# An encoder trunk on one core: the MLP's first product takes both parts of the activations as one 512-column operand

## The chip, the core and the metric

The kernel runs on one core of a Trainium2 chip. The metric is the device time of one launch in microseconds. TensorE (PE in the profile; its weight loads are PEld) multiplies into PSUM, ScalarE (ACT) and VectorE (DVE) read PSUM and work on SBUF, GpSimd (POOL) does small work on SBUF, and SyncE (SP) issues the DMAs that bring the weights in from HBM.

## The reference, cut to what matters

Two layers (`DEPTH` = 2) over 256 tokens of width 1024: four token mixers with gates, then an MLP with 4096 hidden features. The change is in the MLP.

```python
for l in range(DEPTH):
    h = rms_norm(x, norm1_g[l])
    ...                                   # projections, four mixers, gates
    x = x + jnp.sum(g * y, axis=2) @ w_o[l]

    h2 = rms_norm(x, norm2_g[l])
    x = x + jnp.square(jax.nn.relu(h2 @ w_ff1[l])) @ w_ff2[l]
return rms_norm(x, final_g)
```

## The kernel before

**Products of split numbers.** Every large product is made of three float32r matmuls: each operand is split into a high part (rounded to float32r) and a low part (what is left), and hi·hi, hi·lo and lo·hi are added up in PSUM. `split_product` issues the three for each block of 128 contracted features; each takes its stationary operand anew. In the trace the three are lines L1179, L1180 and L1181.

**Weights.** A layer's weights come in 64 chunks (`CHUNKS`) of 1 MB, each in two halves. SP loads a half into `raw` (a ring of two chunks), ACT rounds it into `w_hi` (L572, `split_hi`), DVE subtracts into `w_lo` (L806, `split_lo`), and PE uses the chunk from a ring of four (`RING`). SP may load chunk c's half only when DVE is through with that half of chunk c-2, and ACT may write `w_hi` of chunk c only when PE is through with chunk c-4 (`w_used`). A layer's last chunks stand in the order f1 14, f2 13, f1 15, f2 14, f2 15, and the next layer's chunks 0 and 1 follow.

**The MLP.** There are 16 chunks f1 of 256 hidden features and 16 chunks f2 (`FF_N` = 16). The product in (`mlp_in`) of chunk i has the weights as its stationary operand and the activations `act_hi`, `act_lo` (256 tokens) as the moving one: 2 feature blocks (d) x 8 contraction blocks (kc) x 3 matmuls = 48 matmuls of 256 columns, into one half of a PSUM bank for each d (`bank_w[:, i % 2]`; for chunk 0 `bank_w` and `bank_o`). DVE then makes `relu` (L1036: maximum with 0, times `root_row`, which carries the norm's factor of each token), ACT squares it into `part_hi` (L701), DVE squares it into `sq` (L1042) and subtracts into `part_lo` (L1045). The product out (`mlp_out`) of chunk i adds 24 matmuls of 512 columns into the four banks of `bank_acc`, the sums of the whole layer.

**The order.** It is written out by hand, engine by engine. PE: `mlp_in(0)` (in `mlp_in_first`), a matmul that turns `rstd` into a row (L1420, into `bank_x`), `mlp_in(1)`, `mlp_out(0)`, `mlp_in(2)`, `mlp_out(1)`, ... `mlp_in(15)`, `mlp_out_last`. The last one goes by pieces (two token tiles x two halves of the width, 6 matmuls each): pieces 0 and 1 of chunk 14, then pieces 0 and 1 of chunk 15, then 2 and 3 of chunk 14, 2 of chunk 15, the first transposes of the next layer (`turn_h`, L1190), and piece 3 of chunk 15. In the loop ACT and DVE split chunk f1 i+1, do the MLP work of chunk i, and split chunk f2 i; behind the loop they split f2 15 and then do the MLP work of chunk 15. Then they split chunks 0 and 1 of the next layer, and only then does DVE add the sums to `xs` (`residual`, L845), from which the next norm is made (ACT sums squares, POOL makes `rstd`, DVE and ACT scale into `h`), for which `turn_h` waits.

## Time and profile before

| | us |
|---|---|
| three timed runs: median | 841.54 |
| lowest, highest | 841.27, 841.65 |
| the profiled execution | 843.16 |
| its span, first to last instruction | 841.4 |
| granted TensorE clock over the span | 0.995 of full speed |

The profile shows one execution. It took 843.16 us, 1.76 us over its own span and 1.62 us over the median of the timed runs; durations are read inside the span, and a difference worked out from them is put against either time alike. The busy time of a matmul in the profile overlaps the next one's, so what a matmul costs in a stream is the distance between two starts.

### The profile page before, as it was taken

To read this page: it belongs to the slowest core of one execution; us is meant where nothing else is said; L and a number is where in the kernel's file an instruction comes from. 1 tells how busy PE (TensorE), PEld (TensorE's weight loads), DVE (VectorE), ACT (ScalarE), POOL (GpSimd) and SP (SyncE) were. 2 spreads that over 40 slices of the span, in tenths; PEclk is the share of its full clock that TensorE was granted. 3 is DMA by queue.
4 is the path that set the end of the run, shared out by engine and by line. 5 is a ranking of instruction groups with operands and counts; after the bars stand their busy time and mean duration, and the time that the engine had idled before them with its cause. 6 is when DMAs were issued, how large, how long until landed. Compare 5 with 4: busy or idle time off the path is not lost.

```text
span 841.4 us, 14859 instructions
## 1 busy us (share of the span) xinstructions
PE 821.5 (98%) x5781; PEld 754.2 (90%) x5781; DVE 538.2 (64%) x781; ACT 410.8 (49%) x698; POOL 80.8 (10%) x105
## 2 busy tenths in 40 slices
PE   6899999999999999999999999999999999999997
PEld 6899988999889999999989999889997999999995
DVE  4586665966667556665568756677756865556663
ACT  5345566645465334444364566466454643334442
POOL 4030000202210000000033000002211100000000
PEclk9899999999999999999999999999999999999999
DMA  9566643364337655555566654343353655655541
GB/s 283 179 190 198 175 126 101 103 199 142 110 106 245 200 199 181 178 175 184 184 184 203 214 166 143 125 132 119 114 171 125 212 195 194 199 199 187 170 142 50
DMA packets 100850, 141.09 MB, mean 168 GB/s; under 512 B 4796, under 2 KB 87040, under 8 KB 100800
## 3 DMA queue, kind: packets, MB, share of 16 engines
q1 hardware_dynamic: 99296, 137.12, 51.1%
q0 software_dynamic: 1216, 3.17, 1.6%
q8 instruction: 34, 0.56, 0.3%
q10 hardware_dynamic: 288, 0.11, 0.1%
q14 instruction: 16, 0.13, 0.0%
HBM read 139.33 MB, written 1.05 MB: 167 GB/s over the span
## 4 chain that ended last, share of the span: by engine, by line
PE 79%; issue 12%; POOL 4%; DVE 3%; DMA 1%; ACT 1%; POOLq 0%; ACTq 0%; DVEq 0%
PE bank_w L1179 16%; PE bank_w L1181 16%; PE bank_w L1180 16%; PE bank_acc L1179 8%; PE bank_acc L1180 8%; PE bank_acc L1181 8%; POOL mix L542 3%; PE bank_acc L1275 2%; DVE w_lo L806 1%; PE bank_acc L1287 1%; PE bank_o L1304 1%; DMA raw<-in_w_in 1%; PE bank_w L1171 1%; DMA cst<-in_table 1%; PE bank_x L1252 0%
## 5 line engine op out<-in xcount | busy, mean ns | idle before, releaser
L806 DVE TENSOR_TENSOR w_lo<-raw,w_hi 128x1024 fp32r<-128x1024 f32 (+1 forms) x256 | 308.5, 1254 | 48.2 <-ACT w_hi L572 48.0
L1179 PE MATMUL bank_w<-act_hi,w_hi 128*128 128x256 f32 x1008 | 287.9, 286 | 0.0
L1181 PE MATMUL bank_w<-act_hi,w_lo 128*128 128x256 f32 x1008 | 285.8, 284 | 0.0
L1180 PE MATMUL bank_w<-act_lo,w_hi 128*128 128x256 f32 x1008 | 285.3, 283 | 0.0
L572 ACT ACTIVATE w_hi<-raw 128x1024 fp32r<-128x1024 f32 (+1 forms) x256 | 256.7, 1060 | 29.0 <-DMA raw<-in_w_in 18.4
L1179 PEld LDWEIGHTS bank_w<-act_hi,w_hi 128*128 128x128 f32 x1008 | 191.6, 190 | 7.1 <-ACT big L693 3.1
L1180 PEld LDWEIGHTS bank_w<-act_lo,w_hi 128*128 128x128 f32 x1008 | 190.9, 189 | 1.8 <-issue 0.5
L1181 PEld LDWEIGHTS bank_w<-act_hi,w_lo 128*128 128x128 f32 x1008 | 191.2, 190 | 0.0
L701 ACT ACTIVATE part_hi<-big 128x512 fp32r<-128x512 f32 x32 | 20.2, 633 | 194.2 <-DVE big L1036 191.5
L1179 PE MATMUL bank_acc<-w_hi,part_hi 128*128 128x512 f32 x256 | 100.3, 392 | 0.0
L1180 PE MATMUL bank_acc<-w_lo,part_hi 128*128 128x512 f32 x256 | 100.2, 392 | 0.0
L1181 PE MATMUL bank_acc<-w_hi,part_lo 128*128 128x512 f32 x256 | 99.8, 390 | 0.0
L1036 DVE SCALAR_TENSOR_TENSOR big<-bank_w,root_row 128x512 f32<-128x512 f32 x30 | 20.7, 691 | 117.4 <-PE bank_w L1181 117.4
L1179 PE MATMUL bank_w<-w_hi,act_hi 128*128 128x268 f32 x256 | 75.1, 293 | 5.7 <-ACT qkv L609 5.5
L1181 PE MATMUL bank_w<-w_hi,act_lo 128*128 128x268 f32 x256 | 74.4, 291 | 0.0
L1180 PE MATMUL bank_w<-w_lo,act_hi 128*128 128x268 f32 x256 | 74.2, 290 | 0.0
L693 ACT ACTIVATE big<-bank_w,vec_all 128x256 f32<-128x256 f32 x64 | 26.9, 471 | 84.3 <-PE bank_w L1181 84.3
L542 POOL TENSOR_TENSOR mix<-mix,tmp 128x512 f32<-128x512 f32 x24 | 35.5, 1489 | 255.5 <-DVE tmp L1021 255.2
L1181 PEld LDWEIGHTS bank_acc<-w_hi,part_lo 128*128 128x128 f32 x256 | 48.1, 188 | 10.6
L1179 PEld LDWEIGHTS bank_acc<-w_hi,part_hi 128*128 128x128 f32 x256 | 48.1, 188 | 9.5
L1180 PEld LDWEIGHTS bank_acc<-w_lo,part_hi 128*128 128x128 f32 x256 | 48.0, 188 | 8.9
L1179 PEld LDWEIGHTS bank_w<-w_hi,act_hi 128*128 128x128 f32 x256 | 49.4, 193 | 6.0 <-issue 6.0
(180 smaller groups left out, 987.3 us busy)
## 6 DMA issues: line engine op xcount, KB each, us to landing
raw<-in_w_ff SPq DMA_DIRECT2D x128, 512.0 KB, 4.8
raw<-in_w_gate SPq DMA_DIRECT2D x64, 512.0 KB, 4.7
raw<-in_w_in SPq DMA_DIRECT2D x32, 536.0 KB, 5.6
raw<-in_w_o SPq DMA_DIRECT2D x16, 512.0 KB, 4.5
raw<-in_w_branch SPq DMA_DIRECT2D x16, 256.0 KB, 4.4
raw<-in_w_branch SPq DMA_DIRECT2D x8, 512.0 KB, 4.6
xs<-in_x SPq DMA_DIRECT2D x2, 512.0 KB, 4.6
out_y<-big SPq DMA_DIRECT2D x4, 256.0 KB, 2.1
```

The costliest lines, as they stand in the source:

```text
L542: nc.gpsimd.tensor_tensor(mix[:, k % 4, :], mix[:, k % 4, :], tmp[:, k % 2, :], ALU.add).then_inc(mixed, 1)
L572: nc.scalar.activation(half_view(w_hi, c, h), raw_half(c, h), ACT.Copy).then_inc(w_hi_ready, 1)
L693: ins = nc.scalar.activation(big[:, i % 8, d * SEQ:(d + 1) * SEQ], bank[:, d * SEQ:(d + 1) * SEQ], ACT.Tanh, bias=vec(BG + 2 * i + d, l), ...
L701: nc.scalar.activation(part_hi[:, b, :, :].rearrange("p k s -> p (k s)"), relu[b], ACT.Square).then_inc(u_hi_ready, 1)
L806: nc.vector.tensor_tensor(half_view(w_lo, c, hf), raw_half(c, hf), f32(half_view(w_hi, c, hf)), ALU.subtract).then_inc(w_lo_ready, 1)
L1036: ins = nc.vector.scalar_tensor_tensor(out=relu[b].rearrange("p (d s) -> p d s", d=2), in0=bank_w[:, b, :].rearrange("p (d s) -> p d s", d ...
L1171: nc.tensor.matmul(bank_w[:, 1, 0:P], ident, ident, start=True, stop=True)
L1179: nc.tensor.matmul(dst, s_hi, m_hi, start=first, stop=False)
L1180: nc.tensor.matmul(dst, s_hi, m_lo, start=False, stop=False)
L1181: ins = nc.tensor.matmul(dst, s_lo, m_hi, start=False, stop=last)
L1275: ins = nc.tensor.matmul(bank_acc[:, half, keys], q[:, t * P:(t + 1) * P], k, start=True, stop=True)
L1287: ins = nc.tensor.transpose(bank_acc[:, 2 + b, at:at + P], prob[:, b, t, kt * P:(kt + 1) * P], ident)
```

## The change

Chunk i of the MLP's product in now has 4 half banks instead of 2. `act_hi` and `act_lo` become the two halves of one tile `act[:, kc, m, :]`, so that high and low part of a contraction block lie side by side. `wide_product` then issues two matmuls instead of three: w_hi times both parts (512 columns, a whole bank: the left half gets hi·hi, the right half w_hi·act_lo) and w_lo times the high part (256 columns, onto the left half). Both halves have to be added afterwards. ACT copies the right halves of the two banks into `relu` (`u_copy`), DVE adds the left halves (`u_summed`), and the rest follows from SBUF. The banks of odd chunks are `bank_o` and `bank_x`, so `mlp_in(1)` waits until ACT has copied `root_row` out of `bank_x`. DVE's MLP work is cut in two (`mlp`: add, relu, square; `mlp_lo`: the subtraction), and the splits of f2 chunks stand between the two parts; on ACT they stand between `u_copy` and the square.

```diff
-        act_hi = sb("act_hi", [P, KD, SEQ], F32R)
-        act_lo = sb("act_lo", [P, KD, SEQ], F32R)
+        act = sb("act", [P, KD, 2, SEQ], F32R)
+        act_hi, act_lo = (act[:, :, m, :] for m in range(2))
...
-        bank_w = ps("bank_w", [P, 2, 512])
+        bank_u = ps("bank_u", [P, 4, 512])
+        bank_w, bank_o, bank_x = bank_u[:, 0:2, :], bank_u[:, 2, :], bank_u[:, 3, :]
...
+            def u_copy(i, l, g=0):
+
+                b = i % 2
+                act.wait_ge(w_used, used_count(l, POS["f1", i], g))
+                if i >= 2:
+                    act.wait_ge(u_squared, l * FF_N + 2 * g + (i - 1))
+                nc.scalar.activation(relu[b].rearrange("p (d s) -> p d s", d=2), bank_u[:, 2 * b:2 * b + 2, SEQ:2 * SEQ],
+                                     ACT.Copy).then_inc(u_copied, 1)
...
-                split_hi(POS["f2", 0], l)
+                split_hi_half(POS["f2", 0], 0, l)
                 act.wait_ge(root_turned, l + 1)
                 nc.scalar.activation(root_row[:, :], bank_x[:, 0:SEQ], ACT.Copy).then_inc(root_row_ready, 1)
+                u_copy(0, l)
+                split_hi_half(POS["f2", 0], 1, l)
                 mlp(0, l)
                 with act.Fori(0, MLP_TURNS) as g:
                     for i in (1, 2):
                         split_hi(POS["f1", i] + AHEAD - 1, l, g)
+                        u_copy(i, l, g)
+                        split_hi(POS["f2", i - 1] + AHEAD - 1, l, g)
                         mlp(i, l, g)
-                        split_hi(POS["f2", i - 1] + AHEAD - 1, l, g)
+                u_copy(FF_N - 1, l)
                 split_hi(POS["f2", FF_N - 1], l)
                 mlp(FF_N - 1, l)
...
+                banks = bank_u[:, 2 * b:2 * b + 2, :]
+                u = relu[b].rearrange("p (d s) -> p d s", d=2)
+                dve.wait_ge(u_copied, l * FF_N + 2 * g + (i + 1))
+                nc.vector.tensor_tensor(u, u, banks[:, :, 0:SEQ], ALU.add).then_inc(u_summed, 1)
+                dve.wait_ge(u_summed, l * FF_N + 2 * g + (i + 1))
                 if i == 0:
                     dve.wait_ge(root_row_ready, l + 1)
...
                 dve.wait_ge(relu_ready, l * FF_N + 2 * g + (i + 1))
                 nc.vector.tensor_tensor(sq[b], relu[b], relu[b], ALU.mult).then_inc(u_squared, 1)
+
+            def mlp_lo(i, l, g=0):
...
+                mlp(FF_N - 1, l)
                 split_lo(POS["f2", FF_N - 1], l)
-                mlp(FF_N - 1, l)
+                mlp_lo(FF_N - 1, l)
...
+            def wide_product(dst, sides, start, stop, lo_counts=None):
+
+                for k, (s_hi, s_lo, m) in enumerate(sides):
+                    if lo_counts is not None:
+                        pe.wait_ge(h_lo_ready, lo_counts[k])
+                    first, last = start and k == 0, stop and k == len(sides) - 1
+                    nc.tensor.matmul(dst, s_hi, m.rearrange("p m s -> p (m s)"), start=first, stop=False)
+                    ins = nc.tensor.matmul(dst[:, 0:SEQ], s_lo, m[:, 0, :], start=False, stop=last)
+                return ins
...
+                if i == 1:
+                    pe.wait_ge(root_row_ready, l + 1)
                 if i >= 2:
-                    pe.wait_ge(relu_ready, l * FF_N + 2 * g + (i - 1))
+                    pe.wait_ge(u_summed, l * FF_N + 2 * g + (i - 1))
                 pe.wait_ge(w_lo_ready, lo_count(l, c, g))
-                feature_blocks(bank_w[:, i % 2, :], c)
+                wide_block(i % 2, c, 0)
+                wide_block(i % 2, c, 1).then_inc(w_used, 1)
```

How the engines' rows stand at three places follows, each before and after; what a row waits for is in its brackets.

PE, where layer 0's chunk f1 0 ends and chunk f1 1 begins (the rows with `rstd` turn it into `bank_x`), before:

```order
L1179 MATMUL bank_o<-act_hi,w_hi 128x256
L1180 MATMUL bank_o<-act_lo,w_hi 128x256
L1181 MATMUL bank_o<-act_hi,w_lo 128x256
L1420 MATMUL bank_x<-cst,rstd 128x128 [waits rstd_ready]
L1420 MATMUL bank_x<-cst,rstd 128x128
L1179 MATMUL bank_w<-act_hi,w_hi 128x256 [waits w_lo_ready]
L1180 MATMUL bank_w<-act_lo,w_hi 128x256
L1181 MATMUL bank_w<-act_hi,w_lo 128x256
```

and after:

```order
L1210 MATMUL bank_u<-act,w_hi 128x512
L1211 MATMUL bank_u<-act,w_lo 128x256
L1456 MATMUL bank_u<-cst,rstd 128x128 [waits rstd_ready]
L1456 MATMUL bank_u<-cst,rstd 128x128
L1210 MATMUL bank_u<-act,w_hi 128x512 [waits w_lo_ready,root_row_ready]
L1211 MATMUL bank_u<-act,w_lo 128x256
```

Three rows of 256 columns became one of 512 and one of 256, and the first row of chunk f1 1 has a second wait, on `root_row_ready`.

ACT, from the end of the MLP loop in layer 0 to the first sum of squares of the next norm (rows `w_hi<-raw` of 1024 are chunk f2 15, of 1072 chunks 0 and 1 of layer 1; `part_hi<-big` is the square of chunk 15), before:

```order
L572 ACTIVATE w_hi<-raw 128x1024 [waits landed1_0,w_used]
L572 ACTIVATE w_hi<-raw 128x1024 [waits landed1_1,w_used]
L701 ACTIVATE part_hi<-big 128x512 [waits relu_ready]
L572 ACTIVATE w_hi<-raw 128x1072 [waits landed0_0,w_used]
L572 ACTIVATE w_hi<-raw 128x1072 [waits landed0_1,w_used]
L572 ACTIVATE w_hi<-raw 128x1072 [waits landed1_0,w_used]
L572 ACTIVATE w_hi<-raw 128x1072 [waits landed1_1,w_used]
L582 ACTIVATE qkv,mean<-xs 128x512 [waits x_ready] x2
```

and after:

```order
L703 ACTIVATE big<-bank_u 128x512 [waits u_squared,w_used]
L572 ACTIVATE w_hi<-raw 128x1024 [waits landed1_0,w_used]
L572 ACTIVATE w_hi<-raw 128x1024 [waits landed1_1,w_used]
L710 ACTIVATE part_hi<-big 128x512 [waits relu_ready]
L572 ACTIVATE w_hi<-raw 128x1072 [waits landed0_0,w_used]
L572 ACTIVATE w_hi<-raw 128x1072 [waits landed0_1,w_used]
L572 ACTIVATE w_hi<-raw 128x1072 [waits landed1_0,w_used]
L572 ACTIVATE w_hi<-raw 128x1072 [waits landed1_1,w_used]
L582 ACTIVATE qkv,mean<-xs 128x512 [waits x_ready] x2
```

The copy L703, which waits for PE's last `mlp_in` (`w_used`), now stands ahead of the split of f2 15.

DVE at the same place (L845 and L858 are `residual`), before:

```order
L806 TENSOR_TENSOR w_lo<-raw,w_hi 128x1024 [waits w_hi_ready] x2
L1036 SCALAR_TENSOR_TENSOR big<-bank_w,root_row 128x512 [waits w_used]
L1042 TENSOR_TENSOR big<-big 128x512 [waits relu_ready]
L1045 TENSOR_TENSOR part_lo<-big,part_hi 128x512 [waits u_hi_ready,u_squared]
L806 TENSOR_TENSOR w_lo<-raw,w_hi 128x1072 [waits w_hi_ready] x4
L845 TENSOR_TENSOR xs<-xs,bank_acc 128x512 [waits acc_done] x2
```

and after:

```order
L1046 TENSOR_TENSOR big<-big,bank_u 128x512 [waits u_copied,w_used]
L1050 SCALAR_TENSOR_TENSOR big<-big,root_row 128x512 [waits u_summed]
L1054 TENSOR_TENSOR big<-big 128x512 [waits relu_ready]
L819 TENSOR_TENSOR w_lo<-raw,w_hi 128x1024 [waits w_hi_ready] x2
L1061 TENSOR_TENSOR part_lo<-big,part_hi 128x512 [waits u_hi_ready,u_squared]
L819 TENSOR_TENSOR w_lo<-raw,w_hi 128x1072 [waits w_hi_ready] x4
L858 TENSOR_TENSOR xs<-xs,bank_acc 128x512 [waits acc_done] x2
```

The split of f2 15 moved from ahead of the last chunk's work to between its square and its subtraction, and an addition stands in front.

## Rows read from the trace of the kernel before

**Rows 1.** page, head and section 1: busy us, share, instructions
```profile
span 841.4 us, 14859 instructions
...
PE 821.5 (98%) x5781; PEld 754.2 (90%) x5781; DVE 538.2 (64%) x781; ACT 410.8 (49%) x698; POOL 80.8 (10%) x105
```

**Rows 2.** PE timeline: start us, us, engine, line, op, tiles; in the MLP loop
```profile
303.16 0.29 PE L1181 MATMUL bank_w<-act_hi,w_lo 128*128 128x256 f32 x1
303.29 0.40 PE L1179 MATMUL bank_acc<-w_hi,part_hi 128*128 128x512 f32 x1
...
308.54 0.40 PE L1181 MATMUL bank_acc<-w_hi,part_lo 128*128 128x512 f32 x1
308.77 0.29 PE L1179 MATMUL bank_w<-act_hi,w_hi 128*128 128x256 f32 x1
...
314.54 0.40 PE L1179 MATMUL bank_acc<-w_hi,part_hi 128*128 128x512 f32 x1
```

**Rows 3.** timeline of PE: 512 columns meet 256 ahead of the MLP loop
```profile
245.32 0.39 PE L1181 MATMUL bank_acc<-w_hi,act_lo 128*128 128x512 f32 x1
245.55 0.28 PE L1179 MATMUL bank_w<-act_hi,w_hi 128*128 128x256 f32 x1
245.67 0.27 PE L1180 MATMUL bank_w<-act_lo,w_hi 128*128 128x256 f32 x1
```

**Rows 4.** timelines of PEld, PE, ACT in layer 1: `rstd` turned, next chunk, `root_row` copied
```profile
660.04 0.30 PEld L1420 LDWEIGHTS bank_x<-cst,rstd 128*128 128x128 f32 x2 [0.29 <-POOL rstd L498]
...
660.51 0.36 PE L1179 MATMUL bank_w<-act_hi,w_hi 128*128 128x256 f32 x1
...
660.79 0.38 ACT L762 ACTIVATE root_row<-bank_x 128x256 f32<-128x256 f32 x1 [0.68 <-PE bank_x L1420]
```

**Rows 5.** timeline of DVE over the end of layer 0's MLP
```profile
407.10 4.63 DVE L806 TENSOR_TENSOR w_lo<-raw,w_hi 128x1024 fp32r<-128x1024 f32 x4 [0.19 <-ACT w_hi L572]
416.02 0.69 DVE L1036 SCALAR_TENSOR_TENSOR big<-bank_w,root_row 128x512 f32<-128x512 f32 x1 [4.28 <-PE bank_w L1181]
416.74 0.69 DVE L1042 TENSOR_TENSOR big<-big 128x512 f32<-128x512 f32 x1
417.48 0.69 DVE L1045 TENSOR_TENSOR part_lo<-big,part_hi 128x512 fp32r<-128x512 f32 x1
418.40 4.83 DVE L806 TENSOR_TENSOR w_lo<-raw,w_hi 128x1072 fp32r<-128x1072 f32 x4 [0.23 <-ACT w_hi L572]
423.15 1.28 DVE L845 TENSOR_TENSOR xs<-xs,bank_acc 128x512 f32<-128x512 f32 x2
```

**Rows 6.** timeline of ACT over the same stretch
```profile
406.03 3.89 ACT L572 ACTIVATE w_hi<-raw 128x1024 fp32r<-128x1024 f32 x4
416.74 0.63 ACT L701 ACTIVATE part_hi<-big 128x512 fp32r<-128x512 f32 x1 [6.83 <-DVE big L1036]
```

**Rows 7.** timeline of PE over the same stretch
```profile
415.82 0.40 PE L1179 MATMUL bank_acc<-w_hi,part_hi 128*128 128x512 f32 x1
...
426.74 0.33 PE L1190 MATMUL bank_o<-cst,big 128*128 128x128 f32 x1 [1.08 <-DVE big L813]
```

**Rows 8.** SP timeline (DMA issues), then that of ACT: `w_in` loads landing
```profile
438.43 1.55 SPq L421 DMA_DIRECT2D raw<-in_w_in  x2
...
442.25 1.10 ACT L572 ACTIVATE w_hi<-raw 128x1072 fp32r<-128x1072 f32 x1 [1.91 <-DMA raw<-in_w_in]
444.71 1.10 ACT L572 ACTIVATE w_hi<-raw 128x1072 fp32r<-128x1072 f32 x1 [1.36 <-DMA raw<-in_w_in]
```

**Rows 9.** timeline of DVE at the end of layer 1's MLP
```profile
828.24 0.69 DVE L845 TENSOR_TENSOR xs<-xs,bank_acc 128x512 f32<-128x512 f32 x1 [2.07 <-PE bank_acc L1181]
```

**Rows 10.** groups by line: a PSUM bank copied by ACT, 128x512
```profile
L670 ACT ACTIVATE probT<-bank_acc 128x512 f32<-128x512 f32 x32 | 17.4, 596 | 13.3 <-PE bank_acc L1287 13.3
```

**Rows 11.** windows: length, busy us PE PEld DVE ACT POOL, PEclk, DMA share, GB/s
```profile
18.00:24.00 6.00, 1.71 (x14) 1.50 (x13) 3.01 (x3) 1.41 (x2) 0.61 (x1) 1.00 1.09 334
24.00:31.00 7.00, 5.79 (x26) 5.83 (x27) 1.62 (x2) 1.12 (x3) 0.00 (x0) 0.51 0.62 176
```

More of the change, by code:

```diff
@@ L332, in trunk_kernel @@
         relu_ready = sem("relu_ready")
+        u_copied = sem("u_copied")
+        u_summed = sem("u_summed")
         u_squared = sem("u_squared")
@@ L999, in mix_lo @@
                 dve.wait_ge(mix_hi_ready, l * 4 + (q + 1))
-                v = [a[:, 2 * q:2 * q + 2, :].rearrange("p k s -> p (k s)") for a in (act_hi, act_lo)]
-                nc.vector.scalar_tensor_tensor(out=v[1], in0=mix[:, q, :], scalar=0.5, in1=f32(v[0]), op0=ALU.mult,
-                                               op1=ALU.subtract).then_inc(mix_lo_ready, 1)
+                v = [a[:, 2 * q:2 * q + 2, :] for a in (act_hi, act_lo)]
+                nc.vector.scalar_tensor_tensor(out=v[1], in0=mix[:, q, :].rearrange("p (k s) -> p k s", k=2),
+                                               scalar=0.5, in1=f32(v[0]), op0=ALU.mult, op1=ALU.subtract).then_inc(mix_lo_ready, 1)
             def branch(n, l, quarters):
@@ L1029, in mlp @@
                 dve.wait_ge(w_used, used_count(l, POS["f1", i], g))
+                banks = bank_u[:, 2 * b:2 * b + 2, :]
[3 more added lines that the diff above has]
+                dve.wait_ge(u_summed, l * FF_N + 2 * g + (i + 1))
                 if i == 0:
                     dve.wait_ge(root_row_ready, l + 1)
-                    for d in range(2):
-                        ins = nc.vector.scalar_tensor_tensor(out=relu[0][:, d * SEQ:(d + 1) * SEQ], in0=first_u[d], scalar=0.0,
-                                                             in1=root_row[:, :], op0=ALU.max, op1=ALU.mult)
-                else:
-                    ins = nc.vector.scalar_tensor_tensor(out=relu[b].rearrange("p (d s) -> p d s", d=2),
-                                                         in0=bank_w[:, b, :].rearrange("p (d s) -> p d s", d=2), scalar=0.0,
-                                                         in1=root_row[:, :].unsqueeze(1).to_broadcast([P, 2, SEQ]),
-                                                         op0=ALU.max, op1=ALU.mult)
-                ins.then_inc(relu_ready, 1)
+                nc.vector.scalar_tensor_tensor(out=u, in0=u, scalar=0.0,
+                                               in1=root_row[:, :].unsqueeze(1).to_broadcast([P, 2, SEQ]),
+                                               op0=ALU.max, op1=ALU.mult).then_inc(relu_ready, 1)
                 dve.wait_ge(relu_ready, l * FF_N + 2 * g + (i + 1))
                 nc.vector.tensor_tensor(sq[b], relu[b], relu[b], ALU.mult).then_inc(u_squared, 1)
+            def mlp_lo(i, l, g=0):
+                b = i % 2
                 dve.wait_ge(u_squared, l * FF_N + 2 * g + (i + 1))
@@ L1112, in _ @@
                 split_lo(POS["f1", 1], l)
-                split_lo(POS["f2", 0], l)
+                split_lo_half(POS["f2", 0], 0, l)
                 mlp(0, l)
+                split_lo_half(POS["f2", 0], 1, l)
+                mlp_lo(0, l)
                 with dve.Fori(0, MLP_TURNS) as g:
@@ L1119, in _ @@
                         split_lo(POS["f2", i - 1] + AHEAD - 1, l, g)
+                        mlp_lo(i, l, g)
+                mlp(FF_N - 1, l)
                 split_lo(POS["f2", FF_N - 1], l)
-                mlp(FF_N - 1, l)
+                mlp_lo(FF_N - 1, l)
                 k, last = 2 * l + 2, ("f2", FF_N - 1)
@@ L1405, in token_sum, with wide_block @@
                 return split_product(dst, sides, start, stop)
+            def wide_block(b, c, d, kcs=range(KD), lo_counts=None):
+                hi, lo = k_view(w_hi, c, KD), k_view(w_lo, c, KD)
+                sides = [(hi[:, kc, d * P:(d + 1) * P], lo[:, kc, d * P:(d + 1) * P], act[:, kc, :, :]) for kc in kcs]
+                return wide_product(bank_u[:, 2 * b + d, :], sides, kcs[0] == 0, kcs[-1] == KD - 1, lo_counts)
             def mlp_in_first(l):
@@ L1412, in mlp_in_first @@
                 left, right = range(0, KD // 2), range(KD // 2, KD)
-                feature_block(first_u[0], c, 0, left, counts[0:KD // 2])
+                wide_block(0, c, 0, left, counts[0:KD // 2])
                 turn_x(k, 3)
-                feature_block(first_u[1], c, 1, left)
-                feature_block(first_u[0], c, 0, right, counts[KD // 2:])
-                feature_block(first_u[1], c, 1, right).then_inc(w_used, 1)
+                wide_block(0, c, 1, left)
+                wide_block(0, c, 0, right, counts[KD // 2:])
+                wide_block(0, c, 1, right).then_inc(w_used, 1)
                 pe.wait_ge(rstd_ready, k * T + T)
```

5 lines of the change are left out of this document (1 added, 4 removed).

## The prediction

> **What bounds the kernel now.** The head of the page says it first: PE is busy for 821.5 of 841.4 us and no other engine for more than 538.2 [rows 1]. So the time is PE's stream of matmuls plus the few places where PE stands still, and the change touches both. For the stream I read PE's timeline, since the mean duration of a matmul there overlaps the next. In the MLP loop a product in begins at 308.77 and the product out behind it at 314.54 [rows 2]: 5.77 us for 48 matmuls of 256 columns, 0.120 each. The product out from 303.29 to 308.77 is 24 matmuls of 512 columns [rows 2]: 0.228 each. Half the columns cost more than half the time: a straight line through the two has a fixed part of 0.120 x 2 - 0.228 = 0.012 us for each matmul.
>
> **The array: what goes.** A contraction block took three matmuls of 256 columns, 0.360 us. It now takes one of 512 and one of 256: 0.228 + 0.120 = 0.348, if either keeps its price beside the other. That is one fixed part less, 0.012 us. There are 32 products in with 16 blocks each, 512 in all: 512 x 0.012 = 6.1 us. The columns stay 768 and the only thing saved is that fixed part. The trace has no stream in which the two sizes alternate, so I bound it by the places where they meet. In the loop the 256 ahead of a 512 takes 303.29 - 303.16 = 0.13 and the 512 ahead of a 256 takes 308.77 - 308.54 = 0.23 [rows 2], 0.36 together: nothing would be saved. But there a chunk of another kind begins, with register work and waits of the loop around it. Where the two sizes meet outside the loop, the 512 takes 245.55 - 245.32 = 0.23 and the 256 behind it 245.67 - 245.55 = 0.12 [rows 3], as in the streams. Those rows are the nearer ones, with waits but no loop, so I take 6.1; the bounds are 0 and, for 0.013 a block, 6.7.
>
> One rule speaks against most of this gain. The rows have 120 and 228 ns a matmul. The Trainium skill ("TensorE: Matmul & The Clock Gate", Back-to-back issue gap) gives the gap between matmuls without their weight loads as N / 2.4 + 2.5 ns, which is 109 and 216; as an estimate by it, three of 256 take 328 ns, the new pair 325, the array would give 1.3 us and the sum below would be +9.2. This trace disagrees with those gaps, so the sum goes by the rows.
>
> Not all of the 6.1 us arrives. The first product in of each layer is followed by the matmul that needs `rstd` (L1420), and PE stood 0.29 us for it, until POOL had made it [rows 4] (in layer 1; layer 0 is alike). POOL sets that moment, so the 16 x 0.012 = 0.19 us of that chunk buy only more waiting: 0.4 us back in two layers.
>
> **A new wait in front of chunk f1 1.** PE went on at 660.51, while ACT copied `root_row` from 660.79 to 661.17 [rows 4]. Now PE waits for that copy. With some 0.05 us to be let go it starts at 661.22, 0.7 us later, in each layer: 1.4 us. Behind PE's wait stands all of its queue. ACT has one weight half less ahead of the copy than before, so the copy is not later. `mlp_out(0)` needs `part_lo` of chunk 0, whose steps now begin behind this copy: 0.6 for the second copy [rows 10], three steps of DVE at 0.73 and a subtraction of 0.7 [rows 5], a split at 1.13 [rows 5], 4.6 us in all, against 5.6 us of PE's product in. Hidden, by 1 us.
>
> **Inside the loop: nothing.** Per chunk ACT gets a copy of 0.60 us [rows 10] and DVE an addition of 0.69 (like L845, also a sum with PSUM, and every other 512-column row of DVE [rows 5]). PE needs the bank again two chunks later and `part_lo` 11 us after the product in has ended. From that end DVE needs 0.2 + 0.6 for the copy, three times 0.73 to the square, two splits at 1.13, and 0.7: ready after 5.9 us. It then has two more splits, and is free at 8.3 of a period of 11.1. The cover is PE's next product out and in, 11 us; without it the whole 5.9 would show. At the end of the MLP it is gone.
>
> **The end of each MLP.** Call S the start of `mlp_out_last`, 415.82 in layer 0 [rows 7]. PE has two pieces of chunk 14, 12 x 0.228 = 2.74 us, and then needs `w_lo` of f2 15 and `part_lo` of chunk 15. Before, f2 15 had been split since 411.7 (407.10 + 4.63, the last two of the four) and `part_lo` was ready at 418.17 = S + 2.35 [rows 5]: hidden, by 0.4 us. Now ACT and DVE come to the split of f2 15 only behind the copy and the square. ACT copies from S + 0.2 (where `relu` began, 416.02 [rows 5]) to S + 0.8, then rounds the two halves until S + 2.8 (0.95 to 1.0 each [rows 6]). DVE adds at S + 0.84, takes the maximum at S + 1.57 and squares at S + 2.3 (0.73 from one dependent step to the next: 416.02, 416.74, 417.48 [rows 5]). Then come the two subtractions of f2 15, at S + 2.9 and S + 4.05 (four took 4.63, 1.13 apart [rows 5]), and `part_lo` from S + 5.2 to S + 5.9.
>
> PE stands still from S + 2.74 to about S + 5.95: 3.2 us. In layer 1 nothing else follows: there `residual` waited 2.07 us for PE [rows 9], so the end simply moves by 3.2.
>
> **Layer 0 has a second link.** DVE must split chunks 0 and 1 of layer 1 before `residual`, which began at 423.15 = S + 7.33 right behind those splits [rows 5] and let PE's transposes start at 426.74, 3.59 later, after 1.08 us of idle PE [rows 7]. PE was not what these steps waited for, DVE was. Chunk 1 goes into the half of `raw` that f2 15 leaves, so its two loads are issued only at S + 4.25 and S + 5.4. Of two such loads in a row, issued within 1.55 us from 438.43, the second near 439.6, the halves were there at 442.25 and 444.71 [rows 8]: 3.8 and 5.1 us after their issues. So the second half lands at S + 10.5, ACT is through at S + 11.6, DVE at S + 12.85, and `residual` starts 5.5 us later than before; the transposes follow at S + 16.4 instead of S + 10.92. That is 5.5 us for layer 0, its own 3.2 among them. PE is busy for 98% of the span [rows 1], so there is no slack behind it that could take this back.
>
> **The sum.** -6.1 + 0.4 + 1.4 + 5.5 + 3.2 = +4.4 us. The profiled execution took 843.16 and would take 847.6; against the median of the timed runs, 841.54, it is 845.9.
>
> **Rivals.** First, the pair costs what meetings in the loop cost: 0.36 a block: the array gives nothing, and the sum is +10.5 less the 0.4 that then isn't lost, 851.6. For it: the loop's own rows [rows 2]. Against it: [rows 3]. By the rule of the Trainium skill quoted above ("TensorE: Matmul & The Clock Gate", Back-to-back issue gap) it would be 850.7.
>
> Second, the next layer's loads don't count. If the halves of chunk 1 land by S + 9, the 5.5 is 3.2 as in layer 1, and the sum is +2.1: 843.7. For it: 3.8 us is possible; against it: the second of two loads took 5.1 [rows 8].
>
> Third, the clock falls in a new gap. PE stands still for 3.2 us and, 7 us later, for another 3.2. In the trace PE did 1.71 us of work from 18 to 24, and from 24 to 31 the granted clock was 0.51, the level of 1.2 GHz, though PE worked again for most of it [rows 11]. At half speed for 7 us, partly in the gap, 3 us are lost: 848.9.
>
> Fourth, on the faster side, the narrow matmul gets cheaper. The fixed part may be a weight load that a 256-column matmul just fails to cover. Then the 256-column matmul whose load ran under 512 columns would take less. The whole must come to under 0.340 us a pair for a gain: 4.4 + 6.1 = 10.5 us over 512 pairs. At 0.334, both fixed parts gone from the pair but one, it is 13.3 us from the array and 838.7. Against it: 512 behind 512 pays the same 0.012 to 0.015 though its load is covered twice over.
>
> Fifth, the change doesn't do what it says (the copy or the addition slower from two banks, DVE the bound in the loop): it takes over 2.8 us a chunk more on DVE to show, four times the 0.69 of one step. No row comes near that.
>
> **How the numbers follow.** The forecast holds 0.58 (its own range 844.3 to 847.5), the dear pair 0.11, the hidden loads 0.11, the clock 0.10, the cheap pair 0.06, something between 840 and 843 without a name 0.04. A range from 843.2 to 851.5 leaves out the cheap pair, the nameless case and half of the dear pair, and is open at neither end to more than 0.06 besides. A measurement of this kernel can tell about 0.2%, 1.7 us, from no change. Faster by more: 0.07, the cheap pair; within: 0.08, the nameless case and the lower edge of the hidden loads; slower: 0.85.
>
> **What the profile after should show.** In the loop, starts 0.228 and 0.120 apart and 5.56 us for a product in. A gap of 0.7 us at the first row of chunk f1 1. In `mlp_out_last` a gap of some 3.2 us behind the twelfth matmul in both layers, released by DVE's `part_lo`; ACT waiting for a landing of `w_in` ahead of the first sum of squares of layer 1, and a second gap of about 3 us in front of the transposes. The granted clock at full speed throughout. It would be wrong if those gaps were missing or if the pair were not 0.348.

## The result, and the profile after

The changed kernel takes **848.55 us** (median of four runs, 848.24 to 849.70) beside 841.55 for the kernel before in the same comparison: a ratio of 1.009, with a 95% interval of 1.0078 to 1.0102. It is 7.0 us slower. The forecast was +4.4.

The profiled execution of after took 848.24 us. The head of its page, and the groups of lines of the product in and the product out (after `|`: busy us and mean ns of one, then the idle time before them and its releaser):

```profile
span 846.5 us, 13933 instructions
...
PE 819.1 (97%) x5269; PEld 728.1 (86%) x5269; DVE 554.9 (66%) x811; ACT 426.5 (50%) x730; POOL 79.7 (9%) x105
...
L1210 PE MATMUL bank_u<-act,w_hi 128*128 128x512 f32 x512 | 181.4, 395 | 0.9 <-ACT root_row L771 0.9
...
L1199 PE MATMUL bank_acc<-w_hi,part_hi 128*128 128x512 f32 x256 | 101.5, 397 | 6.3 <-DVE part_lo L1061 6.3
```

Against [rows 1], PE has 2.4 us less to do and the span is 5.1 us longer. The idle time has names: 6.3 us for `part_lo` in two gaps, 0.9 for `root_row` in two. Neither group had such idle time before.

**The stream.** Timeline of PE in the MLP loop, as [rows 2]:

```profile
300.00 0.39 PE L1210 MATMUL bank_u<-act,w_hi 128*128 128x512 f32 x1
300.23 0.28 PE L1211 MATMUL bank_u<-act,w_lo 128*128 128x256 f32 x1
300.35 0.40 PE L1210 MATMUL bank_u<-act,w_hi 128*128 128x512 f32 x1
...
301.40 0.40 PE L1199 MATMUL bank_acc<-w_hi,part_hi 128*128 128x512 f32 x1
```

Four pairs take 1.40 us, 0.350 each. The whole product in of chunk 15, from 406.59 to 412.20, is 5.61 us for 16 pairs.

**The start of chunk f1 1**, timelines of PEld, ACT and PE in layer 0, as [rows 4]:

```profile
250.17 0.52 PEld L1456 LDWEIGHTS bank_u<-cst,rstd 128*128 128x128 f32 x4 [0.50 <-POOL rstd L498]
...
250.92 0.38 ACT L771 ACTIVATE root_row<-bank_u 128x256 f32<-128x256 f32 x1 [1.63 <-PE bank_u L1456]
...
251.36 0.50 PE L1210 MATMUL bank_u<-act,w_hi 128*128 128x512 f32 x1 [0.47 <-ACT root_row L771]
```

The wait for `rstd` was 0.29 and is 0.50: the shorter first chunk buys waiting. PE then goes on 1.19 us after 250.17, where [rows 4] has 0.47 (660.04 to 660.51): 0.72 more.

**The end of layer 0's MLP**, timelines of PE, ACT and DVE, as [rows 5 to 7]; S is 412.20:

```profile
412.20 0.40 PE L1199 MATMUL bank_acc<-w_hi,part_hi 128*128 128x512 f32 x1
...
418.25 0.77 PE L1199 MATMUL bank_acc<-w_hi,part_hi 128*128 128x512 f32 x1 [3.15 <-DVE part_lo L1061]
...
428.76 0.44 PE L1220 MATMUL bank_u<-cst,big 128*128 128x128 f32 x2 [1.89 <-DVE big L826]
```
```profile
412.40 0.60 ACT L703 ACTIVATE big<-bank_u 128x512 f32<-128x512 f32 x1 [7.99 <-PE bank_u L1211]
412.89 2.00 ACT L572 ACTIVATE w_hi<-raw 128x1024 fp32r<-128x1024 f32 x2
...
422.85 1.10 ACT L572 ACTIVATE w_hi<-raw 128x1072 fp32r<-128x1072 f32 x1 [1.64 <-DMA raw<-in_w_in]
```
```profile
413.10 0.69 DVE L1046 TENSOR_TENSOR big<-big,bank_u 128x512 f32<-128x512 f32 x1 [6.06 <-ACT big L703]
...
415.15 2.35 DVE L819 TENSOR_TENSOR w_lo<-raw,w_hi 128x1024 fp32r<-128x1024 f32 x2
417.43 0.68 DVE L1061 TENSOR_TENSOR part_lo<-big,part_hi 128x512 fp32r<-128x512 f32 x1
...
425.17 1.28 DVE L858 TENSOR_TENSOR xs<-xs,bank_acc 128x512 f32<-128x512 f32 x2
```

Each link is there: copy, split of f2 15, `part_lo` at S + 5.2, PE back at S + 6.05, chunk 1's second half landed at S + 10.6, `residual` at S + 13.0, transposes at S + 16.6. Layer 1 has the same 3.15 us gap, up to 830.02.

**The clock.** Windows of after (length, then busy us of PE, PEld, DVE, ACT, POOL, then the granted clock):

```profile
412.20:418.00 5.80, 2.90 (x14) 2.07 (x12) 4.83 (x6) 4.98 (x6) 0.00 (x0) 1.00 0.08 10
418.00:421.40 3.40, 3.15 (x8) 2.53 (x9) 2.64 (x4) 1.10 (x1) 0.00 (x0) 0.50 0.93 289
...
831.00:834.40 3.40, 3.40 (x9) 2.65 (x8) 0.69 (x1) 0.72 (x2) 0.18 (x1) 0.50 0.00 0
834.40:841.00 6.60, 5.76 (x25) 4.32 (x23) 4.10 (x7) 1.45 (x4) 1.12 (x3) 1.00 0.04 14
```

PE's timeline in layer 1:

```profile
830.02 0.47 PE L1199 MATMUL bank_acc<-w_hi,part_hi 128*128 128x512 f32 x1 [3.15 <-DVE part_lo L1061]
...
831.02 0.63 PE L1200 MATMUL bank_acc<-w_lo,part_hi 128*128 128x512 f32 x1
...
834.43 0.39 PE L1199 MATMUL bank_acc<-w_hi,part_hi 128*128 128x512 f32 x1
```

For 3.4 us the clock was at its lower level, 1.2 GHz: in layer 0 from some 0.25 us before the gap's end, in layer 1 from 1.0 us behind it. The trace of before is at full clock at both places.

**Where the time went**, from the starts of the `rstd` matmuls (x0, x1), of `mlp_out_last` (S0, S1) and of layer 1's first transposes (turn) on PE's timelines, us:

| stretch | before | after | difference | forecast |
|---|---|---|---|---|
| start to x0 | 251.98 | 250.17 | -1.81 | 0 |
| x0 to S0, S1 after x1 (sum of both) | 327.61 | 324.03 | -3.58 | -4.3 |
| S0 to turn | 10.93 | 16.57 | +5.64 | +5.5 |
| turn to x1 | 233.30 | 233.19 | -0.11 | 0 |
| S1 to end | 17.55 | 22.49 | +4.94 | +3.2 |

From x0 on it is +6.89, close to the +7.0 of the timed runs. The first row is chance of the two profiled executions: before's was 1.62 us over its own median and after's 0.31 under its own. The first chunk's own saving of 0.2 a layer is swallowed by the wait for `rstd`, as forecast. Among the kernels below, which differ little or not at all up to there, x0 stands anywhere from 249.5 to 251.9. So stretches are compared below, not spans.

### The profile page after: what moved, and what is told of

Same layout as the page of the kernel before. It is cut to its first block, busy times and chain, and to the rows that moved or that the text cites. A ratio compares the mean times of both kernels' runs of the same rounds, so it can differ in the third digit from the quotient of the medians.

```text
span 846.5 us, 13933 instructions
## 1 busy us (share of the span) xinstructions
PE 819.1 (97%) x5269; PEld 728.1 (86%) x5269; DVE 554.9 (66%) x811; ACT 426.5 (50%) x730; POOL 79.7 (9%) x105
## 4 chain that ended last, share of the span: by engine, by line
PE 77%; issue 12%; POOL 4%; DVE 3%; DMA 2%; ACT 1%; POOLq 0%; DVEq 0%; ACTq 0%
PE bank_u L1210 13%; PE bank_u L1199 9%; PE bank_u L1201 9%; PE bank_u L1200 9%; PE bank_acc L1199 8%; PE bank_acc L1200 8%; PE bank_acc L1201 8%; PE bank_u L1211 7%; POOL mix L542 3%; PE bank_acc L1305 2%; DMA raw<-in_w_in 2%; PE bank_acc L1317 1%; DVE w_lo L819 1%; PE bank_u L1334 1%; PE bank_u L1191 1%
## 5 line engine op out<-in xcount | busy, mean ns | idle before, releaser
L1210 PE MATMUL bank_u<-act,w_hi 128*128 128x512 f32 x512 | 181.4, 395 | 0.9 <-ACT root_row L771 0.9
L1199 PE MATMUL bank_u<-act,w_hi 128*128 128x256 f32 x512 | 148.1, 289 | 0.0
L1201 PE MATMUL bank_u<-act,w_lo 128*128 128x256 f32 x512 | 144.5, 282 | 0.0
L1200 PE MATMUL bank_u<-act,w_hi 128*128 128x256 f32 x512 | 144.5, 282 | 0.0
L1211 PE MATMUL bank_u<-act,w_lo 128*128 128x256 f32 x512 | 144.2, 282 | 0.0
L1210 PEld LDWEIGHTS bank_u<-act,w_hi 128*128 128x128 f32 x512 | 96.1, 188 | 23.5 <-ACT root_row L771 1.3
L703 ACT ACTIVATE big<-bank_u 128x512 f32<-128x512 f32 x32 | 19.1, 598 | 170.9 <-PE bank_u L1211 170.9
L1199 PEld LDWEIGHTS bank_u<-act,w_hi 128*128 128x128 f32 x512 | 97.4, 190 | 5.9 <-ACT big L693 3.1
L1200 PEld LDWEIGHTS bank_u<-act,w_hi 128*128 128x128 f32 x512 | 97.5, 190 | 0.5 <-issue 0.5
L1211 PEld LDWEIGHTS bank_u<-act,w_lo 128*128 128x128 f32 x512 | 96.4, 188 | 1.3
L1201 PEld LDWEIGHTS bank_u<-act,w_lo 128*128 128x128 f32 x512 | 97.4, 190 | 0.0
L1046 DVE TENSOR_TENSOR big<-big,bank_u 128x512 f32<-128x512 f32 x32 | 22.0, 687 | 109.5 <-ACT big L703 109.5
L1199 PE MATMUL bank_u<-w_hi,act 128*128 128x268 f32 x256 | 74.9, 293 | 5.4 <-ACT qkv L609 5.3
L1200 PE MATMUL bank_u<-w_lo,act 128*128 128x268 f32 x256 | 74.2, 290 | 0.0
L1201 PE MATMUL bank_u<-w_hi,act 128*128 128x268 f32 x256 | 74.2, 290 | 0.0
L693 ACT ACTIVATE big<-bank_u,vec_all 128x256 f32<-128x256 f32 x64 | 26.9, 471 | 84.0 <-PE bank_u L1201 84.0
```

Of the source, the lines that this page charges most:

```text
L693: ins = nc.scalar.activation(big[:, i % 8, d * SEQ:(d + 1) * SEQ], bank[:, d * SEQ:(d + 1) * SEQ], ACT.Tanh, bias=vec(BG + 2 * i + d, l), ...
L703: nc.scalar.activation(relu[b].rearrange("p (d s) -> p d s", d=2), bank_u[:, 2 * b:2 * b + 2, SEQ:2 * SEQ], ACT.Copy).then_inc(u_copied, 1)
L1046: nc.vector.tensor_tensor(u, u, banks[:, :, 0:SEQ], ALU.add).then_inc(u_summed, 1)
L1199: nc.tensor.matmul(dst, s_hi, m_hi, start=first, stop=False)
L1200: nc.tensor.matmul(dst, s_hi, m_lo, start=False, stop=False)
L1201: ins = nc.tensor.matmul(dst, s_lo, m_hi, start=False, stop=last)
```

## The experiments

Theory: the end of each MLP costs what the order of DVE's and ACT's queues there makes it cost, above all the split of f2 15 behind the copy and the square; the array gains about 5 us all the same. Rivals: the addition itself makes the gaps; the clock makes the loss; the wide matmul brings nothing. The kernels ran in three batches, each with the kernel before (medians 841.76, 841.48 and 841.37: e1 to e4, e5 to e8, e9 to e11). The stretches are those of the one profiled execution of each kernel. The column S0 to turn was 10.93 before, S1 to end 17.55.

| kernel | median us (range) | ratio, 95% | x0 to S0 | S0 to turn | S1 to end |
|---|---|---|---|---|---|
| e1_split_first | 839.99 (839.68–841.57) | 0.9982, 0.9973–0.9991 | 162.02 | 12.34 | 18.79 |
| e2_before_late_split | 847.23 (846.52–848.83) | 1.0069, 1.0053–1.0084 | 163.77 | 14.86 | 19.55 |
| e3_warm_gap | 848.46 (847.96–852.47) | 1.0082, 1.0069–1.0095 | 162.02 | 17.91 | 22.46 |
| e4_sums_ahead | 846.83 (844.30–849.02) | 1.0068, 1.0051–1.0084 | 162.02 | 14.51 | 20.93 |
| e5_root_bank | 839.05 (838.15–839.93) | 0.9971, 0.9961–0.9981 | 161.28 | 12.34 | 18.78 |
| e6_last_narrow | 837.58 (835.97–839.57) | 0.9956, 0.9944–0.9968 | 161.44 | 10.92 | 17.54 |
| e7_grouped | 837.38 (837.00–840.79) | 0.9954, 0.9941–0.9967 | 161.98 | 10.92 | 17.54 |
| e8_warm_12 | 850.83 (847.20–851.29) | 1.0115, 1.0100–1.0130 | 162.02 | 16.29 | 20.95 |
| e9_narrow_sums_ahead | 837.67 (836.30–839.05) | 0.9953, 0.9938–0.9968 | 161.44 | 11.13 | 17.55 |
| e10_before_sums_ahead | 841.24 (840.58–843.17) | 1.0002, 0.9993–1.0011 | 163.78 | 11.13 | 17.56 |
| e11_after_again | 847.83 (847.04–848.87) | 1.0077, 1.0062–1.0092 | 162.03 | 16.63 | 22.32 |

### e1: the split of f2 15 ahead again

```diff
-                u_copy(FF_N - 1, l)
                 split_hi(POS["f2", FF_N - 1], l)
+                u_copy(FF_N - 1, l)
...
+                split_lo(POS["f2", FF_N - 1], l)
                 mlp(FF_N - 1, l)
-                split_lo(POS["f2", FF_N - 1], l)
                 mlp_lo(FF_N - 1, l)
```

> The changed kernel, but at the end of each MLP ACT and DVE split chunk f2 15 ahead of the copy and the addition of chunk 15, as the kernel before does. Theory (the place of this split makes the gaps): part_lo of chunk 15 is ready at about S + 3.7 instead of S + 5.9 (copy 0.6, three steps of 0.73, one of 0.7), so the gap of PE in mlp_out_last shrinks from 3.15 to about 1.0 us in both layers, the clock stays at full speed there, the loads of layer 1's chunk 1 are no longer late, and the transposes of layer 1 start about 12.0 behind S instead of 16.6. The time falls by 4.5 us in layer 0 and 4.0 in layer 1, to about 840.0 us. Rival (the longer chain of copy and addition makes the gaps, wherever the split stands): gaps stay near 3 us and the time near 848.5.

839.99 us: the theory's number. PE's timeline:

```profile
415.43 0.47 PE L1199 MATMUL bank_acc<-w_hi,part_hi 128*128 128x512 f32 x1 [1.01 <-DVE part_lo L1061]
...
423.85 0.66 PE L1220 MATMUL bank_u<-cst,big 128*128 128x128 f32 x4 [1.25 <-DVE big L826]
```

The gap of 3.15 is 1.01, and the clock stays at full speed behind it. Of 10.6 us that the two ends had gained (5.64 + 4.94), 2.65 are left (1.41 + 1.24). That is what copy and addition cost by themselves. With this order the change is worth having, by 0.18%.

### e2: the kernel before, with the late split

```diff
+                act.wait_ge(w_used, used_count(l, POS["f1", FF_N - 1]))
                 split_hi(POS["f2", FF_N - 1], l)
                 mlp(FF_N - 1, l)
...
                 nc.vector.tensor_tensor(sq[b], relu[b], relu[b], ALU.mult).then_inc(u_squared, 1)
+                if last:
+                    split_lo(POS["f2", FF_N - 1], l)
...
-                split_lo(POS["f2", FF_N - 1], l)
-                mlp(FF_N - 1, l)
+                mlp(FF_N - 1, l, last=True)
```

> The kernel before with one thing alone changed: chunk f2 15 is split late, on ACT only when the product in of chunk 15 has ended, on DVE between the square and the subtraction of chunk 15. No copy, no addition, no wide matmul. Theory: part_lo is ready at about S + 4.5, a gap of 1.8 us in each layer, and layer 1's chunk 1 is loaded late, so the transposes of layer 1 come about 4.1 us later: 841.5 + 4.1 + 1.8 = 847.4 us. Rival (the chain of copy and addition makes the loss, the place of the split nothing): 841.5 to 842.

847.23. Timelines of PE and DVE; S is 414.48:

```profile
419.12 0.47 PE L1181 MATMUL bank_acc<-w_hi,part_hi 128*128 128x512 f32 x1 [1.72 <-DVE part_lo L1048]
...
429.34 0.44 PE L1192 MATMUL bank_o<-cst,big 128*128 128x128 f32 x2 [3.06 <-DVE big L814]
```
```profile
418.29 0.69 DVE L1048 TENSOR_TENSOR part_lo<-big,part_hi 128x512 fp32r<-128x512 f32 x1
...
425.75 1.28 DVE L846 TENSOR_TENSOR xs<-xs,bank_acc 128x512 f32<-128x512 f32 x2
```

Without wide matmul, copy or addition, the order alone makes a gap of 1.72 in both layers and puts `residual` at S + 11.27, and the ends cost 3.93 + 2.00 = 5.9 us. With e1's 2.65 that is 8.6; after's own, less the 1.56 that its clock cost (below), is 9.0. The two causes add up to within 0.4 us, and the order is the larger. Its forecast, 847.4, came true.

### e4: `residual` ahead of chunk 1

```diff
                     split_lo(0, l + 1)
-                    split_lo(1, l + 1)
                     residual(k, 0, last)
                     residual(k, 1, last)
+                    split_lo(1, l + 1)
```

(and on ACT the sums of squares ahead of `split_hi(1, l + 1)`).

> The changed kernel, but between the layers the first two residuals on DVE and their sums of squares on ACT stand ahead of the split of layer 1's chunk 1, so they don't wait for its late load. Theory (the second link of layer 0): the residual begins near S + 8.2 instead of S + 13.0, the transposes as soon as PE has done piece 2 of chunk 15, near S + 14.8, so 1.8 us less: 846.7 us. Rival (the late load isn't what the transposes wait for): 848.5, the gap of 1.9 us in front of the transposes stays.

846.83. Timeline of DVE, with S = 411.73:

```profile
419.93 0.68 DVE L858 TENSOR_TENSOR xs<-xs,bank_acc 128x512 f32<-128x512 f32 x1
...
423.33 2.46 DVE L819 TENSOR_TENSOR w_lo<-raw,w_hi 128x1072 fp32r<-128x1072 f32 x2 [1.78 <-ACT w_hi L572]
425.71 0.48 DVE L826 TENSOR_SCALAR big<-xs,rstd 128x512 f32<-128x512 f32 x1
```

and PE's:

```profile
426.24 0.66 PE L1220 MATMUL bank_u<-cst,big 128*128 128x128 f32 x4 [1.25 <-DVE big L826]
```

`residual` is at S + 8.2 instead of S + 13.0, the transposes at S + 14.51 instead of 16.57. So the late landing of chunk 1 did cost layer 0 time beyond its own gap, 2.06 us of it. The expectation had the transposes wait for PE's own work, near S + 14.8. The place came true and the reason didn't: PE had nothing to do for 1.25 us and waited for DVE's scaling, which stands behind the split of chunk 1. DVE in turn had waited 1.78 us for ACT's rounding of chunk 1, which now comes behind the sums of squares. That is where the rest of the 4.8 went. This execution had the same 3.15 us gaps and no fall of the clock, and its S1 to end is 20.93, 1.56 less than after's, with the same code there. The runs split with the granted clock: 844.30 and 844.76 at 0.996, 846.78 to 849.02 at 0.991 to 0.992.

### e3 and e8: PE kept busy in the gap

```diff
+                keep_warm(22)
                 pe.wait_ge(w_lo_ready, lo_count(l, POS["f2", b]))
                 pe.wait_ge(u_lo_ready, l * FF_N + (b + 1))
```

(matmuls of constants into a bank nobody reads; 12 in e8.)

> The changed kernel with 22 small matmuls on PE (the identity times itself, into a free bank, not part of the result), put into the gap of mlp_out_last, some 2.5 of its 3.15 us. Theory (the granted clock falls in the gap, and in layer 1 the slow matmuls behind it count): the clock stays at 2.4 GHz there, layer 1's end gets 1.7 us shorter, in layer 0 nothing is gained because DVE's residual is waited for: 848.55 - 1.7 = 846.8 us. Rival (the fall of the clock costs nothing, or falls all the same): 848.5.

```profile
416.22 5.07 PE L1191 MATMUL bank_u<-cst 128*128 128x128 f32 x44
421.05 0.48 PE L1199 MATMUL bank_acc<-w_hi,part_hi 128*128 128x512 f32 x1
```

848.46 instead of 846.8: 22 fillers took 4.8 us, longer than the gap, and PE came back 1.5 us late, so the time is no test. The trace shows something all the same. The clock held through the filled gap in both layers, and S1 to end, 22.46, is the 20.93 of e4 and those 1.5 us. In layer 0 it fell behind the second gap, which was 3.15 us long, for 3.4 us from 432.0, and turn to x1 was 234.81, 1.5 us more than in e1, e2 and e4.

> The changed kernel with 12 small matmuls on PE in the gap of mlp_out_last (not part of the result). In e3_warm_gap 22 of them took 4.7 us, 0.213 each, more than the gap; 12 take 2.6 of its 3.15 us. Theory (the granted clock falls in the gap, and slow matmuls behind it cost 1.5 to 1.8 us in layer 1): 848.55 - 1.7 = 846.8 us and full clock around both ends. Rival (the fall costs nothing): 848.5.

850.83: wrong by 4 us. PE's timeline, then windows:

```profile
414.30 2.84 PE L1191 MATMUL bank_u<-cst 128*128 128x128 f32 x24
417.61 0.47 PE L1199 MATMUL bank_acc<-w_hi,part_hi 128*128 128x512 f32 x1 [0.47 <-DVE part_lo L1061]
...
427.84 0.69 PE L1220 MATMUL bank_u<-cst,big 128*128 128x128 f32 x2 [3.06 <-DVE big L826]
```
```profile
411.70:427.30 15.60, 12.60 (x67) 10.32 (x65) 11.06 (x13) 8.52 (x13) 0.93 (x3) 1.00 0.65 200
427.30:430.60 3.30, 2.76 (x11) 2.57 (x12) 2.21 (x6) 2.75 (x10) 0.00 (x0) 0.50 0.18 62
824.40:843.00 18.60, 14.22 (x74) 11.62 (x72) 10.98 (x16) 7.24 (x14) 2.05 (x6) 1.00 0.08 28
```

The first gap was filled and the clock held through it, and in layer 1 through to the end: S1 to end is 20.95 instead of 22.49, as expected. But in layer 0 the second gap was now 3.06 us instead of 1.89, and the clock fell there, where nothing hides it: turn to x1 became 234.57, 1.3 us more. The profiled execution was also the quickest of four, 847.20 at a clock of 0.995; the others took 850.43 to 851.29 at 0.990 to 0.992. One fall of 3.4 us takes 0.002 off the mean clock (half speed for 3.4 of 846 us). So, as an estimate, the others had some two such stretches more; where they were no trace shows.

### e5: `root_row` through a bank of its own

On top of e1, the `rstd` row goes through `bank_acc`, which is free then, and chunk f1 1 waits for nothing:

```diff
-                nc.scalar.activation(root_row[:, :], bank_x[:, 0:SEQ], ACT.Copy).then_inc(root_row_ready, 1)
+                nc.scalar.activation(root_row[:, :], bank_acc[:, 2, 0:SEQ], ACT.Copy).then_inc(root_row_ready, 1)
...
-                if i == 1:
-                    pe.wait_ge(root_row_ready, l + 1)
```

> The kernel of e1_split_first, with rstd's row turned into a bank of bank_acc that is free at that time, so that the product in of chunk 1 needs no wait for the copy of root_row. Theory (the new wait in front of chunk f1 1 costs 0.7 us in each layer): the gap of 0.47 us in front of that chunk is gone in both layers, and the time is 1.4 us less than the 839.99 of e1_split_first: 838.6 us. Rival (the copy's lateness is made up behind it): 840.0.

```profile
250.36 0.71 PE L1456 MATMUL bank_acc<-cst,rstd 128*128 128x128 f32 x4 [0.16 <-POOL rstd L498]
250.83 0.48 PE L1210 MATMUL bank_u<-act,w_hi 128*128 128x512 f32 x1
```

The distance is 0.47, as in [rows 4], and x0 to S0 fell from 162.02 to 161.28 in each layer: the wait was worth 0.74, 1.5 us in all. The median, 839.05 where 838.6 was expected, is 0.9 under e1's, and 0.7 when each is taken against the kernel before of its own batch.

### e6: the last chunk as before

On top of e5, chunk 15's product in has three matmuls of 256 columns and needs neither copy nor addition, which ACT and DVE leave out for this chunk:

```diff
+                if i == FF_N - 1:
+                    feature_block(bank_u[:, 2, 0:SEQ], c, 0)
+                    feature_block(bank_u[:, 3, 0:SEQ], c, 1).then_inc(w_used, 1)
+                    return
```

> The kernel of e5_root_bank, with the product in of chunk 15 alone made of three matmuls of 256 columns into half banks, as before, so that neither copy nor addition stands ahead of its relu. Theory (the gap of 1.0 us left in mlp_out_last is the copy and the addition): the gap is gone in both layers, 1.2 to 1.4 us each, less 0.2 us for the dearer product of two chunks: 2.3 us less than e5_root_bank, 836.3 us. Rival (another wait takes its place, DVE's splits for the next layer in layer 0): 837.4.

837.58, **0.44% faster than before** (interval 0.32% to 0.56%) and 10 to 11 us faster than the changed kernel. DVE's timeline has the steps of [rows 5] again at the same distances (`relu` at S + 0.2, `residual` at S + 7.3, with S = 413.29), and both ends are back at 10.92 and 17.54:

```profile
413.49 0.69 DVE L1050 SCALAR_TENSOR_TENSOR big<-bank_u,root_row 128x512 f32<-128x512 f32 x1 [3.24 <-PE bank_u L1201]
...
420.61 1.28 DVE L857 TENSOR_TENSOR xs<-xs,bank_acc 128x512 f32<-128x512 f32 x2
```

By stages it gains 2.40 + 2.33 = 4.7 us over the kernel before; the medians show 3.9, on six runs that scatter over 3.6. The expectation is half a hit: by stages e6 is 2.3 us under e5, the theory's number, and both gaps are gone; by the medians it is 1.5 us under, and 837.58 lies at the rival's 837.4. No wait took the gap's place in the trace, so the mechanism is the theory's.

### e7: all wide matmuls of a block, then all narrow ones

```diff
-                    nc.tensor.matmul(dst, s_hi, m.rearrange("p m s -> p (m s)"), start=first, stop=False)
-                    ins = nc.tensor.matmul(dst[:, 0:SEQ], s_lo, m[:, 0, :], start=False, stop=last)
+                    nc.tensor.matmul(dst, s_hi, m.rearrange("p m s -> p (m s)"), start=start and k == 0, stop=False)
+                for k, (s_hi, s_lo, m) in enumerate(sides):
+                    ins = nc.tensor.matmul(dst[:, 0:SEQ], s_lo, m[:, 0, :], start=False, stop=stop and k == len(sides) - 1)
```

> The kernel of e6_last_narrow, with the wide products in another order: first the matmuls of 512 columns of a bank, then its matmuls of 256, instead of by turns. The same matmuls, the same loads of weights. Theory (what lost 0.02 to 0.03 us a chunk and d against the sum is that the sizes alternate: 0.233 for a 512 ahead of a 256 instead of 0.227): a product in takes 16 x (0.227 + 0.120) = 5.55 us instead of 5.61, 30 of them 1.7 us less, 834.6 us. Rival (the 0.233 comes from what is read or written, not from the turns): no difference, 836.3.

```profile
299.44 2.03 PE L1209 MATMUL bank_u<-act,w_hi 128*128 128x512 f32 x8
301.31 1.12 PE L1211 MATMUL bank_u<-act,w_lo 128*128 128x256 f32 x8
302.27 0.40 PE L1199 MATMUL bank_acc<-w_hi,part_hi 128*128 128x512 f32 x1
```

Eight wide ones take 1.87 us, 0.234 each, eight narrow ones 0.96, 0.120 each: 0.354 a pair against 0.350. The median is that of e6; the stretches are a little longer, x0 to S0 161.98 against 161.44. So grouping gains nothing and costs 0.5 us a layer; that the sizes alternate isn't what makes the wide one dear, and the rival's reading was right.

### e9 and e10: e4's order where there is no gap

The edit of e4, on e6 (e9) and on the kernel before (e10).

> The kernel of e6_last_narrow with the first two residuals between the layers and their sums of squares ahead of the split of layer 1's chunk 1. Theory (DVE's splits for the next layer, not PE, set the start of the transposes, in this kernel as in the one before): the idle of 1.08 us in front of the transposes goes to nothing and all else stays: 1.1 us less than e6_last_narrow, 836.5 us. Rival (the scaling, now behind the split of chunk 1 on DVE, is late instead): 837.6 or more.

> The kernel before with the same reordering between the layers and nothing else, no wide matmul. Theory: the idle of 1.08 us in front of the transposes goes here too, 841.5 - 1.1 = 840.4 us. With e9_narrow_sums_ahead it prices the wide product alone: 30 products in at 5.61 instead of 5.77 us each, 4.9 us between the two. Rival (the array's gain of the wide form is lost elsewhere): they differ by less than 2 us.

837.67 and 841.24 where 836.5 and 840.4 were expected: neither gains, and e9's rival was right. S0 to turn is 11.13 in both, not less than 10.92. In e9's DVE timeline the two additions came to stand early, and then DVE had nothing for 1.78 us, split chunk 1, and scaled behind it:

```profile
417.16 1.48 DVE L857 TENSOR_TENSOR xs<-xs,bank_acc 128x512 f32<-128x512 f32 x2
420.43 2.46 DVE L818 TENSOR_TENSOR w_lo<-raw,w_hi 128x1072 fp32r<-128x1072 f32 x2 [1.78 <-ACT w_hi L572]
422.80 0.48 DVE L825 TENSOR_SCALAR big<-xs,rstd 128x512 f32<-128x512 f32 x1
```

In e9 too PE waited for that scaling, 1.29 us. So the idle of 1.08 us in [rows 7] isn't to be had by this reordering: the split comes before the additions or before the scaling, and DVE is late either way.

Their difference is the array's gain without the losses at the ends, expected at 4.9: 2 x (163.78 - 161.44) = 4.7 us by stages, 3.6 by the medians. The rival, under 2 us, is refuted. The six runs of e9 fall into two groups, 836.30 to 836.52 and 838.82 to 839.05; the profiled one is of the second, and 1.35 us of its excess stands between turn and x1. Against the first group the difference of the medians would be 4.8.

### e11: the changed kernel again

> The changed kernel once more, on the chip of the other two. 848.5 us as before, with a granted clock near 0.991 over the span. If in some executions the clock doesn't fall in the gap of layer 1, these are some 1.6 us shorter, at a clock near 0.995.

Its windows, to be set beside those of after:

```profile
418.00:421.40 3.40, 3.40 (x15) 2.78 (x16) 2.46 (x3) 1.10 (x1) 0.00 (x0) 1.00 1.00 319
829.40:832.90 3.50, 3.04 (x7) 2.51 (x8) 0.34 (x2) 0.00 (x0) 0.00 (x0) 0.51 0.00 0
```

847.83 where 848.5 was expected, at a clock of 0.991 in one run and 0.994 in three. The same kernel, the same gap of 3.15 us in layer 0, and no fall there; S0 to turn is 16.63 all the same, against 16.57 with the fall: in layer 0 PE is early anyway (a second gap of 3.41 instead of 1.89). In layer 1 it fell, and S1 to end is 22.32. So no execution of the kind that the expectation asked for, without a fall in layer 1, was traced here; the price of that fall comes from e4 and e8.

## Why the prediction was right or wrong

**Direction, mechanism and places: right.** Two gaps behind `part_lo`, a wait for `root_row`, and a second link through chunk 1's landing were forecast and are in the trace; e1, e2, e4, e5 take each away or make it alone. The range held the time, but 848.55 lies 2.6 us above the forecast and outside its own 844.3 to 847.5. It lies beside the third rival's 848.9; that nearness is luck, since the rival's 3 us are twice what the clock cost, and the rest came from the array.

**The array: 5.1 instead of 5.7 net of the first chunks.** The step that failed is "0.228 + 0.120 = 0.348, if either keeps its price beside the other", and the term -6.1 that rests on it. The pair is 0.350 to 0.351. The 15 chunks behind x0 save 163.84 - 161.28 = 2.56 us (e5), 0.17 a chunk, where 0.19 was taken. The narrow one kept its 0.120, the wide one takes 0.231 instead of 0.228. The 0.36 read where the two sizes meet in the loop, which I had set aside, was indeed farther off than the 0.348. The cause of the 0.003 is open; e7 rules out the alternation. The Trainium skill's rule ("TensorE: Matmul & The Clock Gate", Back-to-back issue gap) gave, as an estimate by it, 1.3 us; the traces disagree, with 5.1. (The +9.2 worked out from it still holds the whole 0.4 for the first chunks; with a saving of 2.5 ns a block that is under 0.1, and the sum +8.9.)

**The 0.4 for the first chunk: right.** The wait for `rstd` grew from 0.29 to 0.50.

**`root_row`: right.** 0.7 forecast, 0.74 by e5.

**The loop: right.** From chunk f1 1's first row at 251.36 to S PE waits for nothing that the trace shows; `part_lo` of chunk 0 was hidden too.

**Layer 0's end: right.** PE back at S + 6.05 (forecast 5.95), landing S + 10.6 (10.5), `residual` S + 12.97 (12.85), transposes S + 16.56 (16.4): +5.64 for 5.5. The rival by which the loads don't count is refuted by e4, where taking the late load out from ahead of `residual` gave 2.06 back. Its sum was wrong besides: with the halves landed by S + 9 the prediction's own links put `residual` at S + 11.35, 4.0 us late and not 3.2; it would have needed S + 8.2.

**Layer 1's end: +4.94 instead of +3.2.** The gap and what belongs to it is 3.38 (20.93 - 17.55, from e4, where the clock held). The other 1.56 is the clock: eight matmuls, from 831.02 to 834.43, at 0.43 instead of 0.23. The forecast said "the granted clock at full speed throughout", and put the fall into a rival at 0.10. It happened, on top of the forecast and not instead of it, at half that rival's price: it lasted 3.4 us and not 7, and layer 0's fell where PE would have stood for DVE anyway. The weighing that failed: [rows 11] shows a fall with 1.7 us of work in 6, and the new gap of 3.2 us looked short beside it.

Together: +4.4, 0.6 that the array saved less and 0.1 that `root_row` cost more, 1.6 for the clock, 0.3 for the rest of the two ends, and -0.1 between turn and x1: +6.9.
